# Three slices of the SSD input projection multiplied by quarters, with the seven additions ahead of the convolution

## The reference

```python
y = conv_general_dilated(x, w[:, None, :], padding=[(2, 2)], feature_group_count=channels) + b
xbc = silu(y)
xs, bm, cm = split(xbc, [1536, 2048])      # 12, 4 and 4 tiles of 128 channels
```

## Time and profile before

| | us |
|---|---|
| median of 3 runs | 2084.59 |
| lowest and highest | 2082.59, 2087.24 |
| the profiled execution, its own time | 2082.04 |
| its span | 2080.1 |
| PE busy | 1904.1 (92%) |
| DVE busy | 652.0 (31%) |
| ACT busy | 399.4 (19%) |
| POOL busy | 252.1 (12%) |
| mean granted clock of PE, as a share of 2.4 GHz | 0.965 |

### The profile page before, as it was taken

One profiled execution on the slowest core, in us unless ns is written; L12 is line 12 of the kernel. 1 busy time (PEld: TensorE's weight loads), 2 busy tenths in 40 slices (PEclk: granted clock), 3 DMA queues, 4 the chain that ended last, 5 costly groups with the idle time before them and its releaser, 6 DMA issues.

```text
span 2080.1 us, 19811 instructions
## 1 busy us (share of the span) xinstructions
PE 1904.1 (92%) x8310; PEld 906.7 (44%) x8310; DVE 652.0 (31%) x1149; ACT 399.4 (19%) x717; POOL 252.1 (12%) x268
## 2 busy tenths in 40 slices
PE   8999999999999997999888988988988988988987
PEld 4656554466678853333333333333333333333332
DVE  6599747588864443001000100100100100100103
ACT  1434313189910021000000000000000000000001
POOL 1786500055400000000000000000000000000001
PEclk9999999999999998999999999999999999998999
DMA  5622303143332486999999999999999999999995
GB/s 149 139 82 67 115 14 128 54 152 122 122 142 91 171 346 250 406 426 435 430 430 429 435 433 430 430 430 434 431 433 431 429 432 432 431 432 430 431 424 245
DMA packets 78953, 638.14 MB, mean 307 GB/s; under 512 B 19933, under 2 KB 33681, under 8 KB 60817
## 3 DMA queue, kind: packets, MB, share of 16 engines
q1 hardware_dynamic: 66224, 628.99, 73.7%
q10 hardware_dynamic: 12640, 7.89, 1.3%
HBM read 626.98 MB, written 9.88 MB: 306 GB/s over the span
## 4 chain that ended last, share of the span: by engine, by line
PE 50%; DMA 38%; DVE 2%; ACT 2%; issue 0%; SPq 0%; DVEq 0%
PE ps L1078 49%; DMA arena<-in_w_e 38%; ACT arena L727 1%; ACT L727 0%; PE ps L1555 0%; PE ps L1189 0%; DVE arena L2192 0%; PE ps L1252 0%; DVE arena L2157 0%; PE ps L1306 0%; DVE arena L2186 0%; DVE arena L2092 0%; DVE arena L2094 0%; PE ps L1443 0%; PE ps L1414 0%
## 5 line engine op out<-in xcount | busy, mean ns | idle before, releaser
L1078 PE MATMUL ps<-arena 128*64 128x512 f32 (+9 forms) x7712 | 1827.0, 528 | 135.6 <-DMA arena<-in_w_e 120.5
L1078 PEld LDWEIGHTS ps<-arena 128*64 128x64 f32 (+2 forms) x7712 | 834.6, 159 | 1095.4 <-issue 917.5
L727 ACT ACTIVATE arena<-ps 128x512 f32<-128x512 f32 (+5 forms) x314 | 174.9, 582 | 1563.5 <-PE ps L1078 973.8
L2157 DVE TENSOR_TENSOR arena<-arena,ps 128x512 f32<-128x512 f32 (+1 forms) x48 | 30.3, 645 | 685.1 <-PE ps L1078 685.1
L719 POOL TENSOR_TENSOR arena<-arena 128x1024 f32<-128x1024 f32 x3 | 7.0, 2348 | 1348.4 <-ACT arena L727 1348.4
L2166 DVE TENSOR_TENSOR arena<-arena,ps 128x512 f32<-128x512 f32 x48 | 33.1, 690 | 408.5 <-PE ps L1078 408.5
L727 ACT ACTIVATE arena<-arena 128x128 f32<-128x128 f32 (+10 forms) x261 | 117.7, 509 | 71.9 <-DVE arena L2116 19.0
L727 ACT ACT_TABLE_LOAD x74 | 94.9, 1283 | 23.3 <-issue 21.6
L1870 DVE SCALAR_TENSOR_TENSOR arena<-arena 128x512 f32<-128x512 f32 x80 | 63.5, 794 | 2.8
L679 POOL TENSOR_TENSOR arena<-arena 128x768 f32<-128x768 f32 x16 | 28.5, 1781 | 181.3 <-PE ps L1252 130.4
L1555 PE MATMUL ps<-arena 128*128 128x128 f32 x176 | 25.8, 295 | 7.0 <-DVE arena L2157 5.9
(11 more groups left out here) (208 smaller groups left out, 713.0 us busy)
## 6 DMA issues: line engine op xcount, KB each, us to landing
arena<-in_w_e SPq DMA_DIRECT2D x76, 5632.0 KB, 29.0
arena<-in_w_e SPq DMA_DIRECT2D x15, 2816.0 KB, 25.9
arena<-in_w_e SPq DMA_DIRECT2D x26, 1408.0 KB, 15.0
arena<-in_w_in SPq DMA_DIRECT2D x9, 2048.0 KB, 8.6
arena<-in_w_e SPq DMA_DIRECT2D x12, 1536.0 KB, 16.8
arena<-cumulative_scratch SPq DMA_DIRECT2D x16, 768.0 KB, 4.9
arena<-in_w_in SPq DMA_DIRECT2D x5, 1536.0 KB, 6.4
arena<-in_w_out_ssd SPq DMA_DIRECT2D x4, 1536.0 KB, 7.2
```

What stands on the lines that cost most here:

```text
L727: return act.activation(out, in_, func, **kw)
L1078: return pe.matmul(out, lhsT, rhs, start=a, stop=z)
L2157: tt(o, o, ps[:, 3 + i, 0:w], ALU.mult).then_inc(s.hid_ready, 1)
```

## The change

Slice 0 and slice 1 stay as they are. Slices 2, 3 and 4 are each one product of a 512 x 1024 matrix with a 1024 x 512 matrix, and this is cut in quarters: channels in two halves, tokens in two halves, the contraction in two halves. Seven products, each of two channel tiles by 256 tokens by 4 k-tiles (8 matmuls of 256 columns), go to six banks in turn (`channel_bank`).

- POOL forms the four block differences of `xT` once (`x_sums`), when the S5 stage no longer needs the place, and four sums of weight blocks (`w_sums`) for each of the three slices. Each is 128 x 1024 elements from SBUF to SBUF. Those of slice 2 start when its weights have landed; those of slices 3 and 4 wait also for products 2, 3 and 5 (counted from 0) of the slice before, which read the old sums. All stand ahead of `differences(0)` in POOL's list.
- ACT no longer copies the tiles of slices 2 to 4 into `xraw`; it copies the first product of each (`one_product`), in its list behind the convolution of tile 2 of the slice before.
- DVE adds the other six products up in seven additions (`upper_channels`, `lower_channels`), each of 128 x 512 with one operand in PSUM. All seven stand ahead of the four tiles of the slice's convolution, and behind the convolution of the slice before.
- PE waits for a bank by the addition that read it last, and for the sums from POOL. The release of a weight slot counts seven products instead of four tiles.

```diff
+            pool.wait_ge(s.F_ps, GP)
+            ...
+            for k, (x, y) in enumerate(((b01, b00), (b11, t_[0]), (b11, b01), (t_[1], b10))):
+                ...
+                pool.tensor_tensor(t_[k], x, y, sub).then_inc(s.terms_ready, 1)
+            for b in range(2, XBC // 512):
+                i = FIRST_XBC + b
+                pool.wait_ge(slice_loaded[i % NW], 16 * (i // NW + 1))
+                ...
+                if b > 2:
+                    pool.wait_ge(s.xbc_ps, channels_done(b - 1, 2))
+                pool.tensor_tensor(s_[0], a10, a11, ALU.add).then_inc(s.terms_ready, 1)
+                pool.wait_ge(s.terms_ready, n0 + 1)
+                pool.tensor_tensor(s_[1], s_[0], a00, sub).then_inc(s.terms_ready, 1)
+                pool.wait_ge(s.terms_ready, n0 + 2)
+                if b > 2:
+                    pool.wait_ge(s.xbc_ps, channels_done(b - 1, 3))
+                pool.tensor_tensor(s_[3], a01, s_[1], sub).then_inc(s.terms_ready, 1)
+                if b > 2:
+                    pool.wait_ge(s.xbc_ps, channels_done(b - 1, 5))
+                pool.tensor_tensor(s_[2], a00, a10, sub).then_inc(s.terms_ready, 1)
@@ ACT
+                    if j == 2 and 1 <= b < XBC // 512 - 1:
+                        one_product(b + 1)
@@ PE
+                for n_, (x, y, term) in enumerate(((a00, b00, 0), (s_[1], t_[1], n0 + 2), (s_[0], t_[0], 0), (s_[3], b11, n0 + 3),
+                                                   (a01, b10, 0), (s_[2], t_[2], n0 + 4), (a11, t_[3], 0))):
+                    ...
+                    for h_ in range(2):
+                        for k in range(KT // 2):
+                            r = mm(channel_product(b, n_)[:, h_, :], x[:, k, P * h_:P * h_ + P], y[:, k, :], k == 0, k == KT // 2 - 1)
+                    r.then_inc(s.xbc_ps, 1)
@@ DVE
+            def upper_channels(b):
+                ...
+                dve.wait_ge(s.xbc_ps, channels_done(b, 1))
+                dve.wait_ge(s.one_copied, b - 1)
+                tt(upper, one_sum, p6, ALU.add).then_inc(s.xbc_raw, 1)
+                ...
+                tt(right, upper, p5, ALU.add).then_inc(s.xbc_raw, 1)
+                ...
+                tt(right, right, p3, ALU.add).then_inc(s.xbc_raw, 1)
+                dve.wait_ge(s.xbc_ps, channels_done(b, 4))
+                tt(left, one_sum, p2, ALU.add).then_inc(s.xbc_raw, 1)
+            def lower_channels(b):
+                ...
+                dve.wait_ge(s.xbc_ps, channels_done(b, 5))
+                tt(upper, upper, p7, ALU.add).then_inc(s.xbc_raw, 1)
+                ...
+                tt(right, upper, p5, ALU.add).then_inc(s.xbc_raw, 1)
+                dve.wait_ge(s.xbc_ps, channels_done(b, 6))
+                tt(left, upper, p4, ALU.subtract).then_inc(s.xbc_raw, 1)
             for b in range(XBC // 512):
                 ...
                 for j in range(4):
                     i = 4 * b + j
+                    if b >= 2 and j == 0:
+                        upper_channels(b)
+                        lower_channels(b)
```

More of the change, by code:

```diff
@@ L269, in encoder @@
         bT, cT = S.take(GROUPS, SEQ), S.take(GROUPS, SEQ)
+        S2 = Space(arena, S.at, top)
+        x_sums, w_sums = S2.take(4, KT // 2, SEQ // 2), S2.take(4, KT // 2, SEQ // 2)
+        S2 = Space(arena, S.at + 2 * TT * GI + 4 * (TT - 1) * GI + 2 * GI, top)
+        upper, one_sum = S2.take(2, SEQ // 2), S2.take(2, SEQ // 2)
         zg_odd, zg_even = S.take(TT, GI), S.take(TT, GI)
@@ L340, in quarter, with channel_product, channel_blocks @@
             return buf[:, 2 * r:2 * r + 2, HALF * q:HALF * q + HALF]
+        channel_bank = (5, 6, 7, 0, 1, 4)
+        channels_done = lambda b, n=6: 4 + 7 * (b - 2) + n + 1 if b >= 2 else 4 * b
+        sums_done = lambda b, n=6: 4 + 7 * (b - 2) + n + 1
+        freed_by = (None, 0, 5, 2, 3, 4, 6)
+        def channel_product(b, n):
+            return ps[:, channel_bank[(7 * (b - 2) + n) % 6], :].rearrange("p (t w) -> p t w", t=2)
+        def channel_blocks(b):
+            half = KT // 2
+            w = wring[:, (FIRST_XBC + b) % NW]
+            return ([[w[:, half * k:half * k + half, 256 * r:256 * r + 256] for k in range(2)] for r in range(2)],
+                    [[xT[:, half * k:half * k + half, 256 * q:256 * q + 256] for q in range(2)] for k in range(2)])
         quarters = ((1, 1), (0, 0), (0, 1), (1, 0))
@@ L873, in _, with one_product @@
             gelu(NQ - 1)
+            def one_product(b):
+                act.wait_ge(s.xbc_ps, channels_done(b, 0))
+                if b > 2:
+                    act.wait_ge(s.xbc_raw, sums_done(b - 1, 3))
+                f(one_sum, channel_product(b, 0), ACT.Copy).then_inc(s.one_copied, 1)
             def conv_gates(b):
@@ L1233, in _ @@
                     w = slice_wait()
-                    for j in range(4):
+                    if b >= 2:
+                        channel_products(b)
+                    for j in range(4 if b == 1 else 0):
                         i = 4 * b + j
@@ L1362, in _ @@
             w = slice_wait()
-            pe.wait_ge(s.xbc_raw, 16)
+            pe.wait_ge(s.xbc_raw, sums_done(XBC // 512 - 1, freed_by[1]))
             z_tile(0, 0, w)
+            pe.wait_ge(s.xbc_raw, sums_done(XBC // 512 - 1))
             pe.wait_ge(s.silu_done, 17)
@@ L1407, in mix_transposed @@
                 if c == 0:
-                    pe.wait_ge(s.one_copied, 5)
+                    pe.wait_ge(s.one_copied, XBC // 512 - 2 + 5)
                 else:
```

63 lines of the change are left out of this document (48 added, 15 removed).

## The result

| | before | after |
|---|---|---|
| median of the runs, us | 2084.61 (12 runs) | 2089.91 (12 runs) |
| lowest and highest | 2081.55, 2087.24 | 2088.37, 2094.91 |
| the profiled execution, its own time | 2082.04 | 2089.95 |
| PE busy | 1904.1 | 1897.8 |
| DVE busy | 652.0 | 676.7 |

The ratio of the medians is 1.0028 [1.0020, 1.0036]: slower by 0.28%, 5.3 us. That is inside the range, but not the forecast (2086.4): it is where the prediction put its rival, the backlog (2089.5). PE is busy for 6 us less, and the kernel is slower.

A forecast was written before the change was run, and what follows sets the result against it. It took the chain through PE's slices and the work behind them as the bound: PE's saving, less start delay and longer tail, gave +1.8 us on the 2084.59 median, so 2086.4 us, range 2082.4 to 2090.5.

The forecast's parts named there:

- the backlog: Rival at slice 0's last tile and slices 1, 2 on DVE: three sums get in, +4.9 us, 2089.5; chance 0.20.
- Step 1: PE, slices 2 to 4: 24.27 us each for 27.68, plus 0.35 for each of two transposes; products end at 405.1.
- Step 2: POOL's added sums: x sums cost nothing in DVE's idle time; each weight sum costs a waiting DVE tap 2.1 us.
- Step 3: Slice 0's last convolution tile: weights land at 319.5, two sums get in, slice 2 starts 1.8 us later.
- Step 4: DVE in slices 2 to 4: 25.8 us of work against 24.3 plus 2.05, just enough; slack 1 to 4 us.
- Step 5: Behind slice 4's last product: an addition, four convolution tiles and 2.3 us of POOL interference; convolution ends 3.0 us later.
- Step 6: Behind the last convolution: DVE 1.6 us later after using 1.4 of slack, PE 1.8 later; the later holds, +1.8.
- if the first sum catches the tap: Backlog rival's condition: a sum starting before the tap at 319.57 lets three sums in, +3.9 us at the start.
- the one through PE: Rival: the SSD stage's start hangs on PE's products, not the convolution; up to 9.1 us saved, 2075.5; chance 0.07.

The follow-up runs named there:

- the split with late sums: Changed kernel, each slice's last three additions behind its second convolution tile and slice 2's POOL sums held until slice 0's convolution is done: 2088.45 us.
- PE kept busy: Changed kernel plus twelve unread matmuls of 384 columns on PE ahead of its wait for the last SiLU: 2090.55 us.
- the additions split: Changed kernel with the last three of a slice's seven additions moved between its second and third convolution tile: 2085.05 us.
- the last slice plain: Changed kernel with slice 4 multiplied as before, copied and convolved tile by tile, slices 2 and 3 by quarters: 2080.06 us.
- its three relatives: Slice 4 multiplied as before, plus slice 2's sums held behind slice 0's convolution (2079.52 us), additions split too (2081.06), or additions split only (2080.01).
- the last slice plain and the sums held back: Changed kernel with slice 4 multiplied as before and slice 2's POOL sums waiting until slice 0's convolution is done: 2079.52 us.

## Why the prediction was right, and which terms were off

The range held the time, and what acted were the mechanisms that the prediction named; but the forecast was 3.5 us too low, and what it called the backlog, by three sums in the first tile, is what happened. The time is inside the range because its high end was taken from that rival. By the prediction's own chances, which count the backlog as slower and not as within, the outcome had 0.21.

That the rival's number, 2089.5, is only 0.4 from the median is in part luck. It has 3.9 us for the start, 1.1 for a low clock that lasts longer ahead of slice 2, and -0.1 for the rest. Measured are 3.2 for the start, 0.1 for the clock (slice 2's records take 1.31 us more than the next slice's, and 1.23 in before), and 1.9 for the rest, where the terms were too low for the transposes (0.9 with the rounding) and behind the last convolution (1.5), and too high for the tail (0.4).

- **Step 1, PE.** 24.39 us for a slice against 24.27 forecast: right. The 0.35 us for each of the transposes ahead of slice 4 did not come: from one slice's transposes to the next pass 26.57 us against 29.90, 3.33 less and not 3.76. Two slices: 0.9 us off.
- **Step 2, the price of a sum.** 2.1 us forecast, 1.97, 1.98 and 1.62 measured. The nearest rows in kind were the right ones to lean on. What a sum costs depends on where it stands when the tap is due: each of the three taps ends 0.56 us behind the end of its sum (323.62 and 324.18, 326.39 and 326.95, 328.80 and 329.36). By the Trainium skill ("SBUF — State Buffer", "Who interferes with whom") the engine that comes second is blocked for the whole instruction of the other; the trace agrees with that to the 0.20 us by which 0.56 is less than a tap's own 0.76. The x sums cost nothing, as said, but not for the reason given: they ran ahead of DVE's idle time, beside instructions that they did not lengthen.
- **Step 3, the count.** This is the step that failed: "so two sums get in before the tile ends". The landing was right to 0.1 us, 12.05 after the convolution's start and 12.15 forecast. But the second tap would have started at 12.22, 0.17 us behind the sum, and not ahead of it: three sums got in, +3.2 us and not +1.8. The prediction's own two numbers already had it so, a landing at 319.5 and a tap at 319.57, and its count took the other order. It had the case as its rival, "if the first sum catches the tap". A count that turns on 0.1 us should not have had a chance of 0.20 only.
- **Step 4, DVE keeps up.** Right: no product waits for DVE. Slack was thin, as said: slice 2's last addition waits 2.05 us for PE and slice 3's 1.70, and the split with late sums uses it up.
- **Step 5, the tail.** 17.55 us forecast, 17.12 measured.
- **Step 6, what is late next.** This failed too. Taking 1.4 us of DVE's slack off and 1.2 us off PE assumed that the SSD stage would absorb part of the delay. It absorbed none: from the last convolution's end to the fourth L1889 pass 14.52 us before and 14.80 after. PE took 9.95 us behind the last SiLU (428.83 to 438.78), where 8.5 were forecast: 22 records on the chain and not 20, and for the clock 2.5 us and not 2.0 (24 records in 10.54 us, against 8.01 in the run with PE kept busy). The 2.0 was read too low to begin with: in before's execution the low clock cost slice 2 1.2 us (28.91 against 27.68) and the two groups of transposes 1.8 (3.91 against 2.15), together 3.0 and not 1.1 and 0.9. DVE's wait of 1.39 us became 1.89. Even without PE's lateness only 0.7 us would have been had, as the run with PE kept busy shows (1.05 in the run with the additions split): DVE's own chain of L1913, L1897 and L1889 behind the last SiLU is nearly as long.

The sum against measurement: the last convolution was forecast 3.0 us later and is 4.8 later (the third sum 1.4, the transposes and rounding 0.9, the tail -0.4), the stage behind it was forecast to give 1.2 back and took 0.3. Together that is the 3.3 us between +1.8 and +5.1.

What the rivals got right: the one through PE (2075.5) needed the tail not to grow. The run with the last slice plain makes exactly that so for two slices, and lands at 2080.06, faster than both kernels; so do its three relatives, 2079.52 to 2081.06, and between these four the runs don't decide.

## What to carry to other kernels

When an engine's work is cut into parts that all have to be in before the next engine can start, it is the last piece of a stage that pays: price the last slice by itself, as products saved against consumer work moved behind the last product. Here it saves 3.3 us and costs 11.5, while the two slices before it keep their 3.3 each. A helper instruction whose result nobody needs yet is not free if it shares a resource with a chain that somebody waits for; and two repairs that each work can starve each other where both draw on the same slack, so run them together before adding their gains. Filling an idle engine helps only if nothing later lived on the filler, and only as far as the other engine's chain is shorter.

## What the runs showed of the hardware

- DVE and POOL take turns, instruction by instruction. A tap of 0.76 us beside a 1024-element sum on POOL of 2.33 to 2.69 us takes 2.38 to 2.74, beside a 512-element one 1.65. A tap that is due while a sum runs ends 0.56 us behind it, so it loses the rest of the sum less 0.20 us.
- How the turn is handed on can be counted: a chain of dependent taps met one sum for each tap, so half as long a sum made each tap lose half as much (0.9 and not 2.0 us), and the number of sums that fall on a chain matters as much as their length.
- It is not only the taps, which have two inputs in SBUF. The tensor_scalar L1979, with one SBUF tensor and a column of coefficients, took 2.58 us beside the fourth sum, in place of 0.54, and 1.49 beside a half sum. The additions with one input in PSUM keep their 0.68 us beside a sum (L1943 at 347.73, with POOL's L725 from 347.34 to 350.04), and so do DVE's S5 instructions beside the x sums. The Trainium skill ("SBUF — State Buffer", "Who interferes with whom") counts a DVE instruction with one SBUF input as free of contention, unless it runs in a two-port mode, which it says a tensor_scalar can enter; whether this one ran in such a mode no run shows.
- PE's clock fell after idle times of very unlike length: 9.06 us, but also 1.61 us at the start of the SSD loop in one execution (the last slice plain and the sums held back: 0.50 from 432 to 438), where before had the same 1.61 us and kept the full clock. From the fourth L1889 to the mixing stage the loop takes 282.5 us in ten of the profiled executions of this document, and 283.7 (twice) or 285.3 and 285.4 in the four whose clock fell in it.
